# Where the sliding-window units stand among a head's key steps

## What is computed

```python
h = _rms_norm(x, norm_g[layer]) * (1.0 + scale[:, None, :]) + shift[:, None, :]
(qa, ka, va, fa, za, qb, kb, vb, zb, ga, gb) = jnp.split(h @ w_in[layer], offsets, axis=-1)
ya = _fox_attention(qa, ka, va, log_f)   # 8 heads x 64, causal, decay by cumulated log f
ya = (ya * jax.nn.silu(za)) @ w_o_fox[layer]
yb = _swa_attention(qb, kb, vb, sinks)   # 8 query heads, 2 key heads, window of 2 chunks of 64
yb = (yb * jax.nn.silu(zb)) @ w_o_swa[layer]
merged = jax.nn.sigmoid(ga) * ya + jax.nn.sigmoid(gb) * yb
x = x + gate[:, None, :] * (merged @ w_out[layer])
```

## Time and profile before

| | |
|---|---|
| median of 3 runs | 2040.95 us (2038.14 to 2043.18) |
| profiled execution | 2040.65 us, of which the traced span is 2038.8 us |
| TensorE busy over the span | 1926.0 us, 94% |
| ScalarE, GpSimd, VectorE busy | 727.6, 547.8, 918.2 us |
| mean granted TensorE clock | 0.979 of full speed |
| attention stage | about 1086 to 1659 us of the span |

### The profile page before, as it was taken

How to read it: one execution, slowest core, us unless ns; L and a number is a source line. 1 busy time by engine, 2 the same in 40 slices (tenths; PEclk the granted TensorE clock), 3 DMA queues, 4 the chain that set the end, 5 groups by cost and what they waited for, 6 DMA issues and landing times. The chain is left out here.

```text
span 2038.8 us, 27725 instructions
## 1 busy us (share of the span) xinstructions
PE 1926.0 (94%) x9722; PEld 1544.3 (76%) x9722; DVE 918.2 (45%) x1931; ACT 727.6 (36%) x1335; POOL 547.8 (27%) x502
## 2 busy tenths in 40 slices
PE   7698999999999999999997889999999989999998
PEld 2577878788887887888885666667766669998887
DVE  1652565646522122210225556767676456555333
ACT  1561222222201122321204567787778770012100
POOL 1431000000000000000003567777778752110000
PEclk9699999999999999999998899999999999999999
DMA  7322243434444122121416256466646334233321
GB/s 248 114 83 96 83 125 93 123 93 144 145 103 129 47 93 82 50 88 46 142 42 144 53 119 159 106 143 149 135 108 140 103 116 135 83 103 122 105 104 72
DMA packets 236591, 222.69 MB, mean 109 GB/s; under 512 B 54738, under 2 KB 188626, under 8 KB 236468
## 3 DMA queue, kind: packets, MB, share of 16 engines
q1 hardware_dynamic: 223044, 180.95, 32.4%
q0 software_dynamic: 11648, 39.85, 6.1%
q10 hardware_dynamic: 1792, 0.53, 0.1%
HBM read 149.18 MB, written 71.70 MB: 108 GB/s over the span
## 5 line engine op out<-in xcount | busy, mean ns | idle before, releaser
L1361 POOL TENSOR_TENSOR Pl<-PT,Ph 128x512 fp32r<-128x512 f32 (+2 forms) x350 | 417.0, 1216 | 155.6 <-ACT Ph L1461 125.3
L546 PE MATMUL pj<-Wh,hTh 128*128 128x512 f32 (+1 forms) x640 | 244.6, 382 | 11.7 <-DVEq L735 6.7
L450 POOL DMA_DIRECT2D wraw<-in_w_in x72 | 38.6, 536 | 794.6 <-DVE Wl L750 760.1
L546 PE MATMUL pj<-hTh,Wh 128*128 128x512 f32 x640 | 249.7, 390 | 0.6 <-DVE Wl L750 0.3
L547 PE MATMUL pj<-hTl,Wh 128*128 128x512 f32 x640 | 249.1, 389 | 0.0
L548 PE MATMUL pj<-hTh,Wl 128*128 128x512 f32 x640 | 249.1, 389 | 0.0
L548 PE MATMUL pj<-Wh,hTl 128*128 128x512 f32 (+1 forms) x640 | 238.9, 373 | 0.0
L547 PE MATMUL pj<-Wl,hTh 128*128 128x512 f32 (+1 forms) x640 | 238.6, 373 | 0.0
L1454 ACT ACTIVATE PT<-sc 128x512 f32<-128x512 f32 (+2 forms) x350 | 191.7, 548 | 129.0 <-PE sc L1388 34.8
L1149 DVE TENSOR_REDUCE part_max<-mx 128x1 f32<-128x512 f32 (+3 forms) x267 | 159.4, 600 | 119.6 <-PE mx L1106 117.5
L1461 ACT ACTIVATE Ph<-PT 128x512 fp32r<-128x512 f32 (+2 forms) x350 | 207.9, 594 | 11.1
(11 more groups left out here) (263 smaller groups left out, 3711.1 us busy)
## 6 DMA issues: line engine op xcount, KB each, us to landing
qk_scratch<-qThl SPq DMA_DIRECT2D x96, 256.0 KB, 2.7
wraw<-in_w_in POOLq DMA_DIRECT2D x84, 256.0 KB, 4.0
g_scratch<-st SPq DMA_DIRECT2D x64, 256.0 KB, 2.4
gt<-g_scratch SPq DMA_DIRECT2D x16, 1024.0 KB, 7.8
xin<-in_x POOLq DMA_DIRECT2D x16, 512.0 KB, 5.0
wada<-in_w_ada SPq DMA_DIRECT2D x16, 512.0 KB, 6.5
z_scratch<-st SPq DMA_DIRECT2D x32, 256.0 KB, 2.4
Qb<-qk_scratch SPq DMA_DIRECT2D x32, 256.0 KB
```

The costliest lines, as they stand in the source:

```text
L546: nc.tensor.matmul(out, a_hi, b_hi, start=first, stop=False)
L1361: pool.tensor_tensor(Pl[n % NPH][0:rows, 0:w], PT[n % NP][0:rows, 0:w], Ph[n % NPH][0:rows, 0:w].bitcast(F32), ALU.subtract).then_inc(low_ ...
```

## The change

In heads 1 to 7 the four units of a head stood one in the second block, one in the third and two in the fourth. They now stand one in the third block and three in the fourth. Head 0, with all its four units in its last block, is as it was, and so are all instructions; what changes is their order.

```diff
@@ -887,7 +887,7 @@
     for i in range(NB):
         j = i % JB
         key_steps = [(x,) for x in range(JB * j + 1)] + [(JB * j + 1, JB * j + 3), (JB * j + 2,)]
-        units = ((0, 1, 1, 2) if i >= JB else (0, 0, 0, 4))[j]
+        units = ((0, 0, 1, 3) if i >= JB else (0, 0, 0, 4))[j]
         cuts = [len(key_steps) * (m + 1) // (units + 1) for m in range(units)]
         first["f", i] = len(steps)
         for m, tiles in enumerate(key_steps):
```

## The result

The kernel after takes 2055.76 us (median of four executions, 2051.52 to 2056.76), the kernel before beside it 2040.64 us. The ratio on record is 1.006, with a 95% interval of 1.0041 to 1.0078 (the two medians alone give 1.007): slower by more than the noise, where 2031.5 us and a gain were forecast, and outside the range of 2020 to 2046. The profiled execution took 2056.76 us, its span is 2054.9.

The account below looks back on a forecast made before the run. ScalarE's queue was taken as full (66.7 of 67.6 us a settled head), PE nearly so, the start running badly. Terms -3.5 + 1.5 - 6 - 8 + 6 + 4 - 5 + 1.5 = -9.5 us gave 2031.5, range 2020 to 2046.

Parts of the forecast that it names:

- The start: Head 0: -3.5 us at steps 9 to 23 and -6 at tile 2 from shorter `VB` waits and low clock, +1.5 against.
- the late row of tile 0: Head 0: row moved at step 18 instead of 17, its first score staying at PE's step 21; +1.5 us (0 to +3).
- -8 for the moved rows: Tile 2: its 5.19 us wait for moved rows comes when the load burst is nearly over; -8 us with the clock.
- +6 for the keys: Head 1: PE asks for keys near 15.5 us, waits about 4 with a low stretch after; +6 us (+3 to +8).
- The keys in heads 2 to 6: First maximum at place 10 instead of 12 asks for keys earlier; waits cost +4 us in five heads (0 to +12).
- The settled heads' evenness: Heads 2 to 6: ScalarE's rows and unit sums spread more evenly, -1.0 us a head, -5 in all (0 to -7).
- Head 7: Gets tile 14's row on top, 2.1 us on a full ScalarE queue; +1.5 us (0 to +2.2).
- A: Rival: key waits at place 10 pass 2 us in heads 1 to 6, clock falls each time; 2057 us, chance 0.13.
- waits of PE for `Pl` larger than today's: Sign of a wrong forecast: PE waits for `Pl` above 2.8 us a head would mean the evenness argument fails.

Follow-up runs that it names:

- the last run: Kernel before with units (0, 0, 1, 3) in head 1, (0, 0, 2, 2) in head 2, row-moving issues one a step from head 3 on: 2034.84 us, 0.9946.

## Why the prediction was wrong

**The start: right, and undersized.** Head 0 was to lose 3.5 + 6 - 1.5 = 8 us and lost 12.6. The waits for `VB` at steps 11 and 32 are gone, and the late row of tile 0, for which +1.5 stood, shows in no wait. Behind its first ten us, head 0 had 23.8 us at half clock (two of the stretches in the earlier trace rows and one of 6.8 us) and has 10.2. Part of that is luck of the execution: the trace that has head 0 unchanged at 94.8 us has 10.2 us of it too. Of ten other runs with the same tuple in head 1, nine have head 0 at 83 to 86 us, and the one with the maxima further apart has 89.

**Head 1: right.** -8 for the moved rows and +6 for the keys; measured -0.2 in sum instead of -2. The 5.2 us wait is gone, the wait for `Ka` is 4.28 us with 6.8 us at half clock, where "about 4 with a low stretch after" stood.

**The keys in heads 2 to 6: right in sum.** Forecast +4; waits of 4.4 us and up to 1.7 for one low stretch. That it was head 4 with 2.6 us, to which I had given slack, and that a faster ScalarE brings more of it, shows that the slack is PE's pace and not a property of the queue: PE being late by other causes hid it.

**The settled heads' evenness: the step that failed.** It stood at -5, "(0 to -7)", with the words "This is more even". Of the 21.5 us that heads 2 to 6 lost, some 6 are the keys' and their clock; the rest, about 15, stands where I had forecast a gain and allowed no loss. With the keys close, where no settled head waits for `Ka`, these heads still take 18.8 us more than before, so the keys are not the main part. The list behind the step had two holes.
- It held the rows and the sums of units, and not the sums of f blocks at places 0, 3, 10 and 23 (they were in the total of the queue only). With them the tile row at place 3 stands in a clump, which the trace of after shows and the spreading undoes.
- It looked at ScalarE alone. What the lead of three steps must cover is ScalarE's work in a few steps less PE's work in the same steps. The maxima moved too, 13 items in places 36 to 43 and 13 in places 10 to 16 (10 and 9 before), and PE sets the pace just where ScalarE has little; at places 3 to 7 it is the other way round. ScalarE's totals were right (63.1 to 63.7 us in both orders), but its idle time went from about 1 us a head to 3.4 and more, and a full engine that must wait for its work in one stretch can't catch up in the next. The 0 at the end of the range was the real mistake: I bounded the gain by the idle time, and for a loss there was no bound, because a total does not limit how badly two queues with a short lead can be out of step.

Shown are: the loss goes with the settled tuple; waits for the sinks' exponential are not its cause; ScalarE does the same work and stands idle some 3 us more a head; with single issues and without late transfers the loss is 1.1 us instead of 3.6, in one head of one trace. That PE's bunched maxima are what keeps ScalarE waiting, and are the 1.1 us, is argued from where the idle time stands. No run varied the maxima cleanly, so it stays open. Of head 3's 4.3 us, 3.0 are more idle time of PE and 1.2 more busy time for the same 340 matmuls at the same clock. That 1.2 is most likely waiting too: a matmul is shown with 0.39 us where the next can start 0.23 us later, so a start that is late by less than 0.16 us counts as busy.

**Head 7.** +1.5 forecast, +4.1 measured. The extra row is there, at place 3 in the same clump. Its work makes ScalarE's queue 1.2 us longer (57.0 to 58.2); the other 2.7 are idle time, as in the settled heads. With the rows spread, head 7 takes 62.2 us in the new order and 60.9 in the old, 1.3 apart.

**The rivals.** A gave 2057 and came out nearest, and by another mechanism: keys at 6 us a head with a low stretch each. Waits for `Ka` passed 2 us in one settled head of five. My own test, "waits of PE for `Pl` larger than today's", named what came, without a price or a chance.

## What to carry to other kernels

When two engines are both near full and one runs a fixed few steps ahead, write down the work of both for every step, all small items included, and look at the difference over a stretch as long as the lead. An even list of one engine says nothing. Then look in the trace for the idle time of the engine that should be full: most of the loss stands there, whatever the wait lists name. A change of order gets a term for a loss there as well as for a gain, and when an engine gets faster, ask which transfer it now reaches too early. Where a change helps the start and hurts the steady part, try it in the start alone, and let the order turn back over more than one period, since loads follow the old order and their users the new one.

## What the runs showed of the hardware

Issuing a small transfer from ScalarE's queue takes about 0.65 us in a group (four took 2.63 us, two 1.28), and the next exponential began 2.11 us late. Given out one a step, three of a tile's four issues in head 3 lay under a 0.63 us activation; the one that came behind an f block's sums did not, and the next exponential began 0.99 us late. Not every issue costs that much: the sums of an f block took 0.21 us to issue, those of a unit, of the same size, 0.63.

Waits of 2.6 and 4.28 us on PE were next to 3.4 and 6.8 us at half the clock, while a settled head's waits, none above 0.7 us, left it at full speed in every settled head of the kernel before. Short waits are no guarantee: in the last run three settled heads, whose longest wait on PE is 1.0 us, have 3.4 us at half clock each, and other traces with the same spreading and order have none.
